# Attention's value products turned round, and the softmax weights normalised by GpSimd before they are transposed

## The reference

```python
p = _masked_softmax(s, mask)               # exp(s - max) / sum
o_cmp = jnp.einsum('bgrqc,bcgd->bqgrd', p_cmp, v_cmp)
o_sel = jnp.einsum('bgrqnl,bgqnld->bqgrd', p_sel, vs_g)
o_win = jnp.einsum('bgrqk,bkgd->bqgrd', p_win, vwi)
o = gb[..., 0:1] * o_cmp + gb[..., 1:2] * o_sel + gb[..., 2:3] * o_win
return o.reshape(B, S, H * Dh) @ w_out     # layer 1: its one branch, no gate
```

## Time and profile before

| | us |
|---|---|
| median of 3 runs | 774.35 (773.83 to 775.64) |
| the profiled execution, its own time | 771.15 |
| its span in the profile | 769.4 |
| PE busy (share of the span) | 708.3 (92%) |
| DVE busy | 522.0 (68%) |
| ACT busy | 374.7 (49%) |
| POOL busy | 274.7 (36%) |

### The profile page before, as it was taken

One profiled execution on the slowest core, in us unless ns is written; L12 is line 12 of the kernel. 1 busy time (PEld: TensorE's weight loads), 2 busy tenths in 40 slices (PEclk: granted clock), 3 DMA queues, 4 the chain that ended last, 5 costly groups with the idle time before them and its releaser, 6 DMA issues. The chain is left out here.

```text
span 769.4 us, 10825 instructions
## 1 busy us (share of the span) xinstructions
PE 708.3 (92%) x3889; PEld 568.7 (74%) x3889; DVE 522.0 (68%) x940; ACT 374.7 (49%) x696; POOL 274.7 (36%) x261
## 2 busy tenths in 40 slices
PE   4799998989968999989999699989969999999997
PEld 2576768778647888868888486868648888878886
DVE  3357687898466887676766877987567885554544
ACT  3255555676336544433433367776346444444431
POOL 7021211000103997979979432520106960000000
PEclk9999998999988999999999999999989999999999
DMA  8997993030653888884877455801845965555521
GB/s 289 357 375 218 351 374 110 1 111 2 206 177 111 270 270 268 276 277 155 289 268 232 131 171 175 296 31 56 279 159 171 287 207 182 172 179 196 168 106 55
DMA packets 93741, 154.03 MB, mean 200 GB/s; under 512 B 6235, under 2 KB 68320, under 8 KB 93696
## 3 DMA queue, kind: packets, MB, share of 16 engines
q1 hardware_dynamic: 80768, 111.24, 44.1%
q0 software_dynamic: 12928, 42.20, 16.5%
HBM read 151.32 MB, written 1.05 MB: 198 GB/s over the span
## 5 line engine op out<-in xcount | busy, mean ns | idle before, releaser
L1077 DVE TENSOR_TENSOR w_lo<-raw,w_hi 128x1024 fp32r<-128x1024 f32 (+3 forms) x198 | 289.8, 1480 | 138.6 <-ACT w_hi L732 138.1
L732 ACT ACTIVATE w_hi<-raw 128x1024 fp32r<-128x1024 f32 (+3 forms) x198 | 201.7, 1026 | 273.4 <-PE lin L1724 249.7
L1722 PE MATMUL lin<-w_hi,st_hi 128*128 128x512 f32 (+2 forms) x568 | 229.7, 404 | 0.1
L1724 PE MATMUL lin<-w_hi,st_lo 128*128 128x512 f32 (+2 forms) x568 | 220.8, 389 | 0.0
L1723 PE MATMUL lin<-w_lo,st_hi 128*128 128x512 f32 (+2 forms) x568 | 220.5, 388 | 0.0
L600 POOL DMA_DIRECT2D ada_ring<-in_ada_w_dram x80 | 45.4, 568 | 259.3 <-PE sc L1835 222.2
L1722 PEld LDWEIGHTS lin<-w_hi,st_hi 128*128 128x128 f32 x568 | 108.9, 192 | 29.3 <-issue 7.9
L1724 PEld LDWEIGHTS lin<-w_hi,st_lo 128*128 128x128 f32 x568 | 108.5, 191 | 21.7
L1723 PEld LDWEIGHTS lin<-w_lo,st_hi 128*128 128x128 f32 x568 | 108.9, 192 | 19.0 <-issue 0.5
L679 POOL TENSOR_TENSOR pool_acc<-pool_acc,ada_ring 128x1024 f32<-128x1024 f32 x40 | 110.8, 2770 | 3.3
L678 POOL TENSOR_SCALAR ada_ring<-ada_ring,cond_b 128x1024 f32<-128x1024 f32 x40 | 65.5, 1639 | 20.4 <-DMA pool_acc<-in_ada_b_dram 18.7
(11 more groups left out here) (258 smaller groups left out, 870.5 us busy)
## 6 DMA issues: line engine op xcount, KB each, us to landing
raw<-in_ffn_w_in_dram SPq DMA_DIRECT2D x88, 512.0 KB, 4.9
ada_ring<-in_ada_w_dram POOLq DMA_DIRECT2D x80, 512.0 KB, 5.0
raw<-in_ffn_w_out_dram SPq DMA_DIRECT2D x22, 1024.0 KB, 5.0
raw<-in_nsa_w_in_dram SPq DMA_DIRECT2D x10, 1024.0 KB, 12.6
ada_first<-in_ada_w_dram SPq DMA_DIRECT2D x8, 1024.0 KB, 13.0
raw<-in_nsa_cmp_w_dram SPq DMA_DIRECT2D x4, 1024.0 KB, 9.6
raw<-in_nsa_w_out_dram SPq DMA_DIRECT2D x4, 1024.0 KB, 9.6
raw<-in_mla_w_out_dram SPq DMA_DIRECT2D x4, 1024.0 KB, 7.9
```

Source lines behind the costliest of these rows:

```text
L732: nc.scalar.activation(part_of(w_hi, s), raw_part(s), ACT.Copy).then_inc(hi_ready, 1)
L1077: nc.vector.tensor_tensor(part_of(w_lo, s), raw_part(s), part_of(w_hi, s).bitcast(F32), ALU.subtract).then_inc(lo_ready, 1)
L1722: nc.tensor.matmul(bank, a_h, w_h, start=first, stop=False)
L1724: return nc.tensor.matmul(bank, a_l, w_h, start=False, stop=last)
```

## The change

Attention goes by pairs of items (two neighbouring heads): 16 pairs in layer 0, 8 in layer 1. TensorE's step q holds the scores of pair q, the transposes of pair q-2 and the values of pair q-3. Four parts:

- The values become the stationary operand (64 columns) and the transposed weights are streamed, 256 and 128 columns for the two key tiles. The two heads of a pair write the two halves of a bank's partitions, so that a bank holds the output turned, [2 heads x 64] by tokens, which is the form the output product wants. In layer 0 both branches of a group of heads add up in one bank (four pairs a bank); in layer 1 a bank holds two pairs. ScalarE and VectorE split a full bank straight into `st_hi` and `st_lo` (`group_high`, `group_low`). The output transposes, `o0`, `o1`, `nsa_step`, `nsa_add` and `mla_step` go, and the output unit waits for the bank of each two k.
- Since the division now can't follow the product, VectorE makes a factor for each pair behind the maxima of the next pair (`factors`: sum times the gate's denominator, then its reciprocal), and GpSimd multiplies the exponentials by it (`normalise`, four instructions a pair) before they are transposed.
- The compressed weights are normalised the same way (`compressed_weights`, `compressed_normed`), transposed ahead of the third pair, and multiplied into each bank ahead of its first pair (`compressed_values`, two products of 512 columns a bank).
- VectorE's step q holds the splits of output weights (in layer 1 also the copies and norms of the last heads), the maxima of pair q, the factors of pair q-1, the copy of the even item of pair q-2 and, at the end of a bank, `group_low`. ScalarE's step q holds the exponentials of pair q, at the end of a bank `group_high`, and the copy of the odd item of pair q-2.
- Buffers: six of exponentials and four of transposed weights where there were three of each; in layer 0 the score banks are sc0, sc1, lin0, lin1 and the sums lie in lin2, lin3. GpSimd's transfers for conditioning row 2 (layer 0) and 10 (layer 1) are issued behind its normalising.

```diff
@@ gpsimd
-            for seg in (3, 4, 2):
+            def normalise(p, pair0, prob_b):
+                pool.wait_ge(factored, pair0 + p + 1)
+                for j in range(2):
+                    buf = prob_b[(2 * p + j) % 6]
+                    for t in range(T):
+                        cols = buf[:, t * P:t * P + (t + 1) * P]
+                        ins = nc.gpsimd.tensor_scalar(cols, cols, coef[:, p % 3, 2 * t + j:2 * t + j + 1], None, ALU.mult)
+                ins.then_inc(normed, 1)
+            for seg in (3, 4):
                 supply(seg)
+            for t in range(T):
+                compressed_normed(t)
+            for p in range(H):
+                normalise(p, 0, prob)
+            supply(2)
@@ scalar: attention
+                def group_high(k):
+                    act.wait_ge(pv_done, group_count[0] + 1)
+                    group_count[0] += 1
+                    nc.scalar.activation(st_hi[:, 2 * k:2 * k + 2, :].rearrange("p k s -> p (k s)"),
+                                         banks[k % 2][:], ACT.Copy).then_inc(st_high, 1)
...
+                    k = (q - 3) // group - 1
+                    if q >= group + 3 and (q - 3) % group == 0 and k < groups - 1:
+                        group_high(k)
@@ vector
+            def compressed_weights(t):
+                dve.wait_ge(cmp_exped, t + 1)
+                cf = cstat[:, t, :]
+                link(nc.vector.tensor_reduce(cf, tfull[:, t, :].rearrange("p (h c) -> p h c", c=CP), X, ALU.add))
+                cf4 = cf.rearrange("p (r u g) -> p r u g", r=2, u=2)
+                link(nc.vector.scalar_tensor_tensor(cf4, cf4, TINY, gates_by_pair[:, t, :, :, :, 0], ALU.max, ALU.mult))
+                nc.vector.reciprocal(cf, cf).then_inc(cmp_summed, 1)
+            def factors(p, item0, gated):
+                dve.wait_ge(exped, item0 + 2 * p + 2)
...
+                    link(nc.vector.scalar_tensor_tensor(cf, total, TINY, gates_of(p), ALU.max, ALU.mult))
...
+                nc.vector.reciprocal(cf, cf).then_inc(factored, 1)
...
+                for q in range(n_pairs + 3):
+                    before(q)
+                    if q < n_pairs:
+                        if q >= 3:
+                            dve.wait_ge(tp_filled, tp0 + 2 * (q - 3) + 2)
+                        for n in (2 * q, 2 * q + 1):
+                            dve.wait_ge(scored, item0 + n + 1)
...
+                    behind(q)
...
+                    if q >= group + 3 and (q - 3) % group == 0 and k < groups - 1:
+                        group_low(k)
+                group_low(groups - 1)
@@ tensor: attention
+                    for t in range(T):
+                        for u in range(2):
+                            n = 2 * p + u
+                            half = slice(DH * u, DH * u + DH)
+                            ins = nc.tensor.matmul(bank[half, c0 + t * P:c0 + S], v_of(n, t),
+                                                   prob_tb[n % 4][:, t * S:t * P + S],
+                                                   start=(t == 0 and not bank_begun[0]),
+                                                   stop=(t == T - 1 and (m == group - 1 or not bank_begun[0])))
...
+                for q in range(n_pairs + 3):
+                    before(q)
+                    if q < n_pairs:
+                        scores(q)
+                    if 2 <= q < n_pairs + 2:
+                        pe.wait_ge(normed, pair0 + q - 1)
+                        for n in (2 * q - 4, 2 * q - 3):
+                            transposes(tp0 + n, [prob_b[n % 6][:, j * P:(j + 1) * P] for j in range(3)])
+                    if q >= 3:
+                        values(q - 3)
@@ tensor: behind attention (layer 1 alike)
             for _ in range(ARING):
                 ada_chunk()
-            pe.wait_ge(o_steps, 8)
-            for m in range(2):
-                o_batch(o0)(T_O0, m)
-            unit(U_OUT0, OUT0, FOUR, 512, stationary, st_wait(T_O0, o_batch(o0)), EACH)
+            unit(U_OUT0, OUT0, FOUR, 512, stationary, output_wait(ST_O0), EACH)
```

More of the change, by code:

```diff
@@ L108, with count_before, stationary_number @@
 FIRST_PIECES = ((0, 2), (2, 2), (4, 2), (6, 2))
+EVICTIONS = []
+def count_before(owners, n, who):
+    return sum(o == who for o in owners[:n])
+def stationary_number(batch):
+    return count_before(TP_EMPTIED, batch, "st") + sum(n for first, n in EVICTIONS if first <= batch)
 def _batches(n, *who):
@@ L706, in _ @@
                 pool.sem_inc(q_rotated, 1)
+            for p in range(H // 2):
+                normalise(p, H, prob1)
             supply(10)
@@ L784, in high_from_tp @@
                 nc.scalar.activation(dst, tp[batch % 2][:], ACT.Copy).then_inc(st_high, 1)
[L786 to L813, removed]
@@ L1197, in group_norm @@
                 return nc.vector.tensor_reduce(stat[:, 0, n_cols:n_cols + groups], squares_buf, X, ALU.add)
[L1199 to L1229, removed]
@@ L1456, in compressed_output @@
[L1456 to L1464, removed]
-                        dve.wait_ge(cmp_pv, 2 * t + pair + 1)
-                        for u in range(2):
-                            j = 2 * pair + u
-                            cf = cstat[:, t, j * G:(j + 1) * G]
-                            ins = nc.vector.tensor_tensor(
-                                o_view[:, pair, u], bank[:, u * 256:(u + 1) * 256].rearrange(
-                                    "p (g d) -> p g d", g=G),
-                                cf.unsqueeze(2).broadcast_to([P, G, DH]), ALU.mult)
-                        ins.then_inc(cmp_added, 1)
-                dve.wait_ge(cmp_added, 4)
@@ L1518, in _, with output_weights, behind @@
-            output_low(T_O0)
+            def output_weights(q):
+                if q % 2 == 0 and 2 <= q <= 8:
+                    low_to(OUT0 + q // 2)
+            def behind(q):
+                if q < T:
+                    compressed_weights(q)
+                if 1 <= q <= H:
+                    factors(q - 1, 0, True)
+            attention(H, R, 0, T_P0, prob, prob_t, score0, summed0, output_weights, behind)
             low_to(OUT0 + 8)
@@ L1811, in x_batch, with output_wait, wait @@
                                         for k in range(k0, k0 + nk) for t in range(T)])
-            def o_batch(o):
-                def batch(batch0, m):
-                    k0, nk = PIECES[m]
-                    transposes(batch0 + m, [o[:, t, k * P:(k + 1) * P] for k in range(k0, k0 + nk)
-                                            for t in range(T)])
-                return batch
+            def output_wait(st0):
+                def wait(k):
+                    if k % 2 == 0:
+                        pe.wait_ge(st_ready, st0 + k // 2 + 1)
+                return wait
             def st_wait(batch0, batch):
@@ new lines, in attention, with scores, values @@
+            def attention(n_pairs, group, item0, pair0, tp0, st0, q_of, k_of, v_of, prob_b, prob_tb, score, banks,
+                          before, group_start=lambda k, bank: False, abreast=1):
+                def scores(p):
+                    if p >= 2:
+                        pe.wait_ge(maxed, item0 + 2 * p - 2)
+                    for n0 in range(2 * p, 2 * p + 2, abreast):
+                        for t in range(T):
+                            w = (t + 1) * P
+                            for n in range(n0, n0 + abreast):
+                                ins = nc.tensor.matmul(score[n % 4][:, t * P:t * P + w], q_of(n, t),
+                                                       k_of(n, t + 1), start=True, stop=True)
+                                if t == T - 1:
+                                    ins.then_inc(scored, 1)
+                def values(p):
+                    k, m = divmod(p, group)
+                    bank = banks[k % 2]
+                    if m == 0:
+                        if k >= 2:
+                            pe.wait_ge(st_ready, st0 + k - 1)
+                        bank_begun[0] = group_start(k, bank)
+                    pe.wait_ge(*emptied(tp0 + 2 * p))
+                    pe.wait_ge(*emptied(tp0 + 2 * p + 1))
+                    c0 = (p % 2) * S
+                    for t in range(T):
+                        for u in range(2):
[5 more added lines that the diff above has]
+                                                   stop=(t == T - 1 and (m == group - 1 or not bank_begun[0])))
+                    if m == group - 1:
+                        ins.then_inc(pv_done, 1)
+                bank_begun = [False]
+                for q in range(n_pairs + 3):
+                    before(q)
+                    if q < n_pairs:
+                        scores(q)
[5 more added lines that the diff above has]
+                        values(q - 3)
```

293 lines of the change are left out of this document (128 added, 165 removed).

## The result

The changed kernel takes 800.35 us (798.64 to 803.21, four runs) where the kernel before takes 774.39: a ratio of 1.034 (95% interval 1.030 to 1.037). Forecast were 777.0 and a range of 770.5 to 784.0: the sign was right, the size wrong by 23 us.

The account below looks back on a forecast made before the run. TensorE was taken to set the pace, VectorE close behind. Terms +2.1 (layer 0 attention), -2.8, +4.9 (layer 1), -2.0, +.3 (contention) gave +2.5; with +.4 clock, 774.35 + 2.9, rounded to 777.0 us; range 770.5 to 784.0.

Parts of the forecast that it names:

- The loop: Layer 0's attention, fifth to last scores: latency through four engines, GpSimd's step 1.3 us; 34.7 against 34.65, no gain.
- the same chain: Layer 0's loop, scores through maxima, factors, GpSimd, transposes and values to scores two steps later: 5.94 us, 2.97 a step.
- side work: Layer 0's loop: compressed products, weight splits and bank splits, 7.9 us, a quarter reaching the end, entered as 2.
- the fourth: Rival for GpSimd's multiplications: two-input price, or held by VectorE's splits; 2.4 us a pair, total 785, chance .10.
- Rival 1: Loop falls to TensorE's own work if GpSimd's four instructions with hand-overs take under 1.0 us; total 771.0, chance .25.
- TensorE's work: A pair in layer 0's loop: two heads' values .98 us, the pair falling from 2.90 to 2.52.
- Run in: Layer 0's attention up to the fifth pair's scores: gain .8 us, give or take 1.5.
- Run out: Layer 0, last scores to the end of the values: 6.50 us becomes 9.3 to 9.5, loss 2.9.
- Behind attention: First chunk product to the fourth weight slot's end, without small splits and transposes: gains 2.8 us, layer 1 2.0.
- The wait for the chunk: Behind the first weight slot after attention, the next chunk's transfer lands late: a 1.4 us wait, hidden before.
- Layer 1: Layer 1's attention: last scores at 530.0 instead of 529.1, run out 11.3 instead of 7.30; loss 4.9 us.
- Clock: Half speed may go on while TensorE is nearly idle from 137 to 142, ahead of layer 0's loop: +.4 us.

Follow-up runs that it names:

- e1: Changed kernel with GpSimd's four multiplications of a pair carrying a second operation, plus 0.0; 779.15 us, ratio 1.0056 to the kernel before.
- e3: Changed kernel without GpSimd's four multiplications of a pair, wait and signal kept, so the output lacks division and gate; 772.57 us, ratio 0.9968 to the kernel before.
- e9: e1 with layer 1's sums and roots for the last heads' norms moved ahead of the first and second pairs' maxima; 778.04 us.
- e8: e1 with transposes and values one step later and layer 1's last norms ahead of the first two pairs' maxima; 768.31 us.

## Why the prediction was wrong

The step that failed is the one for GpSimd in "The loop": "Such instructions overlap a little back to back; I take 1.3". It measured 2.98, above the 2.8 that I gave as upper end. I scaled a 1024-column row, took the nearest sizes from selects, and didn't ask whether the instruction was the same one: the row's has two operations, the change's one, and the trace before held no TENSOR_SCALAR of GpSimd with one. The right bound from below stood in the earlier trace rows, the one from above didn't.

Put 2.98 into the same chain: 5.94 + 1.68 = 7.62 for two steps, 3.81 a step, 41.9 for eleven, with the 2 us of side work 43.9 against 46.72 measured. Put in 1.64 instead: 6.28 for two steps, 36.5 for the loop, and e1 has 37.17. The two traces also show the chain by itself, where nothing disturbs it; here are scores two steps apart, of the changed kernel (the second are those at 158.87, above), then of e1:

```profile
151.57 0.93 PE L1924 MATMUL sc<-k_pair,q_t 64*128 64x128 f32 x8
```

```profile
149.80 0.93 PE L1925 MATMUL sc<-k_pair,q_t 64*128 64x128 f32 x8
...
155.75 0.93 PE L1925 MATMUL sc<-k_pair,q_t 64*128 64x128 f32 x8
```

That is 7.30 and 5.95 for two steps, and the difference of 1.35 is GpSimd's 2.98 less 1.64. So in layer 0 the chain was right and GpSimd's term mis-sized. A second term was too small: 5.5 times 7.30 is 40.2, so side work and half speed cost 6.6 us of the loop and not 2. Rows for that are the 256-column product, 1.69 instead of 0.92 beside a weight split, and the granted clock, 0.89 in the mean.

Of the rivals the fourth came nearest (its sign "GpSimd instructions over .6" was met), at 785 with 2.4 a pair, still 15 below the measured time. Rival 1's kernel at its best is e3, without any multiplication: 772.57 where 771.0 was its price. That the forecast of 777.0 lies 2 us from e1's 779.15 is in part luck, since e1's loop came out 2.5 longer than forecast and its layer 1 1.5 shorter. Two slips in the working are small: the maxima were read as 1.24 and entered as 1.22, and 774.35 + 2.9 is 777.25.

- *TensorE's work*: 0.80 for two heads' values where 0.98 was taken. A rule of the Trainium skill ("TensorE: Matmul & The Clock Gate", Part 3), that a weight load lies beside running products only where the row group differs, would have made it dearer than 0.98; this trace doesn't show such a cost: weights of the second round are loaded from 158.12 on, while the first products run (from 158.06; the second start at 158.33).
- *Run in*: forecast -0.8; after +1.1, e1 -0.5. *Run out*: forecast +2.9; after +4.5, which is the chain with 1.7 more for GpSimd; e1 +2.7.
- *Behind attention*: forecast -2.8 and -2.0; measured -2.9 and -1.4 (e1 -2.9 and -1.7). The wait for the chunk came, but 0.77 long and not 1.4:

```profile
214.52 0.64 PE L1846 MATMUL sc<-ada_ring,cond_b 128*32 128x256 f32 x8 [0.77 <-DMA ada_ring<-in_ada_w_dram]
```

- *Layer 1*: forecast +4.9 (last scores 0.9 later, run out 4.0 longer); after +14.4 (8.4 and 6.0), e1 +3.4 (0.5 and 2.9). So with GpSimd at 1.64 the forecast is 1.5 too high, and its reason holds only in part: the 3.7 that I put on VectorE's queued work can't be had by moving the norms alone (0.8 in e9), and can with another step (3.8 in e8).
- *Clock*: forecast +0.4. The mean granted clock of the whole execution was 0.947 against 0.971, so 85 us at half speed (1.2 GHz) instead of 45 (twice the missing share, times the span). The stretch foreseen is there, the row 139.00:149.50 above at 0.51, after TensorE had idled for the compressed weights:

```profile
139.31 1.12 PE L1759 MATMUL tp<-ident,tfull 128*128 128x128 f32 x4 [3.79 <-POOL tfull L704]
```

But it came in place of the one before and did not add to it: from 128.0 to 138.2, where the earlier trace rows have 0.50, the changed kernel has 1.00. What is new lies inside the attentions, behind waits for GpSimd: about 10 us in layer 0's loop and 16 in layer 1's attention (0.83 there, 0.76 in its run out), where the kernel before has 1.00. What they cost can't be told from the waiting itself, and stays open.

## What to carry to other kernels

A duration is carried over only from the same instruction: same engine, same operation, same number of operations in it, not only the same name and a similar tile. Where work is moved into a chain from engine to engine, its price counts by the steps that the chain has to run in; one more step of lookahead was worth as much here as an instruction at half the price. And here a queue's odd job (the norms) was moved with profit only once that slack was there.

## What the hardware showed that I had not expected

- GpSimd multiplies a tile by a column of factors 1.6 to 2.5 times faster when the instruction also adds 0.0 than when it doesn't: 0.38 against 0.60 us on 128 columns, 0.48 against 0.92 on 256, 1.117 against 2.84 on 1024.
- Beside a VectorE split with two SBUF operands it is mostly GpSimd that pays in attention: in five of the seven meetings in the changed kernel, the split kept 1.21 us while GpSimd's 256-column product took 1.69 to 2.52 instead of 0.92 (in e1 four of five, 1.48 to 1.75 instead of 0.48); a split that began behind GpSimd's product took 1.53 itself, and in the seventh meeting both were longer (2.05 and, for 128 columns, 1.57). In the network's stretch of the kernel before it was VectorE whose splits went from 1.22 to 1.73.
- The stretch ahead of the first scores, the same work in all of these kernels, took 130.4 to 136.0 us in their traces, one reason why the intervals of four to twelve runs still reach 0.2 to 0.35% to each side.
